# Hybrid DeltaNet and GLA block, merge stage: order of rows, head norms and first up part changed

## What is computed

```python
def merge(o_a, z, o_b, gate, dtype):
    y_a = _merge_heads(_rms_norm(o_a, gdn_norm)) * jax.nn.silu(z)
    y_b = _merge_heads(_rms_norm(o_b, gla_norm)) * jax.nn.silu(gate)
    return (jnp.concatenate([y_a, y_b], axis=-1).astype(w_out.dtype) @ w_out).astype(dtype)
...
x = x + m_lat[2] * y_lat
h_lat = _modulate(_rms_norm(x, norm2[i]), m_lat[3], m_lat[4])
x = x + m_lat[5] * _conv_ffn(h_lat, w_up[i], ffn_conv[i], ffn_conv_b[i], w_down[i], True)
```

## Time and profile before

| what | us |
|---|---|
| median of three runs | 1724.89 |
| lowest and highest | 1723.58, 1726.42 |
| the profiled execution | 1726.9 |
| its span, first to last instruction | 1725.2 |
| PE busy in it | 1642.6 |
| DVE busy | 1217.6 |
| ACT busy | 556.3 |
| POOL busy | 429.1 |

### The profile page before, as it was taken

One profiled execution on the slowest core, in us unless ns is written; L12 is line 12 of the kernel. 1 busy time (PEld: TensorE's weight loads), 2 busy tenths in 40 slices (PEclk: granted clock), 3 DMA queues, 4 the chain that ended last, 5 costly groups with the idle time before them and its releaser, 6 DMA issues.

```text
span 1725.2 us, 20820 instructions
## 1 busy us (share of the span) xinstructions
PE 1642.6 (95%) x8237; PEld 1221.3 (71%) x8237; DVE 1217.6 (71%) x1751; ACT 556.3 (32%) x888; POOL 429.1 (25%) x420
## 2 busy tenths in 40 slices
PE   7999999999999969999899799999999999999997
PEld 2544555886689956565577688888888888787886
DVE  2568877599456658888765469899988888534535
ACT  1533233454043322222544422222222222322432
POOL 4000000220123336656213423333333333200000
PEclk9999999989899979999999899999999999999999
DMA  9275554864388640000312311111111111532342
GB/s 337 79 267 155 162 183 151 250 164 128 86 246 235 195 158 13 25 13 25 128 58 78 116 42 47 47 49 49 49 50 49 49 49 38 219 98 98 98 134 85
DMA packets 202172, 194.23 MB, mean 113 GB/s; under 512 B 41045, under 2 KB 156063, under 8 KB 201948
## 3 DMA queue, kind: packets, MB, share of 16 engines
q1 hardware_dynamic: 194972, 187.40, 34.5%
q10 hardware_dynamic: 6816, 5.24, 1.0%
q0 software_dynamic: 288, 0.27, 0.0%
HBM read 150.77 MB, written 42.11 MB: 112 GB/s over the span
## 4 chain that ended last, share of the span: by engine, by line
PE 49%; DVE 6%; ACT 3%; DMA 2%; issue 2%; POOL 2%; SPq 0%; ACTq 0%; POOLq 0%; DVEq 0%
PE PS L2024 9%; PE PS L2026 9%; PE PS L2028 9%; PE PS L2061 4%; PE PS L2063 4%; PE PS L2065 4%; PE PS L1906 4%; PE PS L1920 2%; DVE Qbd L2306 2%; DMA ogb<-og_spill 1%; POOL xr L1866 1%; PE PS L1963 1%; DVE AT L2322 1%; DVE wolo L2418 1%; DVE oss L2270 0%
## 5 line engine op out<-in xcount | busy, mean ns | idle before, releaser
L2450 DVE SCALAR_TENSOR_TENSOR acc<-PS,fcol,acc 128x945 f32<-128x945 f32 (+2 forms) x176 | 215.2, 1223 | 35.4 <-ACT acc L2147 29.8
L2450 DVE SCALAR_TENSOR_TENSOR act<-PS,fcol,act 128x945 f32<-128x945 f32 (+2 forms) x176 | 215.2, 1223 | 21.6 <-ACT act L2147 16.2
L2024 PE MATMUL PS<-h2hi,whi 128*128 128x512 f32 x704 | 219.9, 390 | 0.0
L2026 PE MATMUL PS<-h2lo,whi 128*128 128x512 f32 x704 | 219.6, 389 | 0.0
L2028 PE MATMUL PS<-h2hi,wlo 128*128 128x512 f32 x704 | 219.6, 389 | 0.0
L389 PE MATMUL PS<-hT,wq 128*128 128x512 f32 (+1 forms) x432 | 163.8, 539 | 0.0
L1860 POOL TENSOR_TENSOR wlo<-wu,whi 128x1024 fp32r<-128x1024 f32 x44 | 106.4, 2420 | 215.8 <-ACT whi L2140 215.7
L2024 PEld LDWEIGHTS PS<-h2hi,whi 128*128 128x128 f32 x704 | 132.4, 188 | 27.4
L2026 PEld LDWEIGHTS PS<-h2lo,whi 128*128 128x128 f32 x704 | 132.4, 188 | 27.4
L2028 PEld LDWEIGHTS PS<-h2hi,wlo 128*128 128x128 f32 x704 | 132.3, 188 | 27.6
L2461 DVE TENSOR_TENSOR wrlo<-wr,wrhi 128x1024 fp32r<-128x1024 f32 x41 | 50.2, 1225 | 129.6 <-ACT wrhi L2221 129.6
(11 more groups left out here) (283 smaller groups left out, 2869.6 us busy)
## 6 DMA issues: line engine op xcount, KB each, us to landing
wm<-in_w_mod_dram SPq DMA_DIRECT2D x24, 1024.0 KB, 7.9
wu<-in_w_up_dram SPq DMA_DIRECT2D x44, 512.0 KB, 3.8
wr<-in_w_down_dram SPq DMA_DIRECT2D x44, 512.0 KB, 3.5
wq<-in_w_in_dram SPq DMA_DIRECT2D x12, 512.0 KB, 9.0
gdn_x_image<-ztile SPq DMA_DIRECT2D x10, 516.0 KB, 9.9
gdn_xt_image<-ztile SPq DMA_DIRECT2D x10, 516.0 KB, 8.3
GR<-gdn_gc_rows SPq DMA_DIRECT2D x20, 256.0 KB, 5.3
gdn_w_image<-Wm SPq DMA_DIRECT2D x20, 256.0 KB, 4.9
```

The costliest lines, as they stand in the source:

```text
L2024: pe.matmul(PS[:, b + half, :], whi[k][u][:, kk, :], h2hi[:, 4 * half:4 * half + 4, kk, :], start=(kk == 0), stop=False)
L2026: pe.matmul(PS[:, b + half, :], whi[k][u][:, kk, :], h2lo[:, 4 * half:4 * half + 4, kk, :], start=False, stop=False)
L2450: tp = v.scalar_tensor_tensor(out=t_[:, r0:r1, c0:c1], in0=up[:, r0 + dr:r1 + dr, c0 + dc:c1 + dc], scalar=tap_col(j, k, f), in1=t_[:, r0: ...
```

## The change

SP asks for the row of tile t+1 in step t, one step sooner than before; the first pair of up weights is asked for one step sooner too. On ACT and DVE the head norm is taken apart. ACT: squares(t+2) stands behind h2_evac(t-2) and ahead of h2hi and of second(t-1); the root of tile t+2 stands behind second(t-1). DVE: the sums of tile t+2 (reduced) stand ahead of second(t-1); reciprocal and scalings (scaled) between gated_y(t+1) and y_low(t+1). Since osq then holds the head squares while second(t-1) runs, the squares of x1, of which only the sum is used, are written to og2's rows 3 and 4 (the first two tiles of the order, read by then) for t < 5 and to osq from there. POOL makes the low part of the first up weights ahead of h2lo(5) and not behind it. PE does up part 0, k = 0, token half 0, ahead of turn2(7), and k = 1 behind it.

```diff
@@ -1745,10 +1745,11 @@
                 sp.wait_ge(s_o2[0], NL)
                 x_row(0)
                 x_row(1)
+                og_row(2)
                 for t in range(2, NL + 2):
-                    if t < NL:
-                        og_row(t)
-                    if t == NL:
+                    if t + 1 < NL:
+                        og_row(t + 1)
+                    if t == NL - 1:
                         sp.wait_ge(s_5y, NL)
                         w_pair(0)
                     sp.wait_ge(s_5a, t - 1)
@@ -1870,10 +1871,10 @@
                     g.tensor_tensor(h2lo[:, TORD[t], :, :], h2T[:, TORD[t], :, :], h2hi[:, TORD[t], :, :], ALU.subtract).then_inc(s_hlp, 1)
                 for t in range(NL):
                     add(t)
+                    if t == NL - 2:
+                        low(0)
                     if t:
                         h2_low(t - 1)
-                    if t == NL - 2:
-                        low(0)
                 low(1)
 
                 def gated(f):
@@ -2014,7 +2015,6 @@
                     project(t, 1)
                     if t:
                         turn2(t - 1)
-                turn2(NL - 1)
 
                 def up(f, k, halves_of):
                     u = f % 2
@@ -2030,9 +2030,11 @@
                     return mm
                 pe.wait_ge(s_hlp, 5)
                 pe.wait_ge(s_5x, NL - 1)
-                for k in range(2):
-                    pe.wait_ge(s_wl[k], 1)
-                    up(0, k, (0,))
+                pe.wait_ge(s_wl[0], 1)
+                up(0, 0, (0,))
+                turn2(NL - 1)
+                pe.wait_ge(s_wl[1], 1)
+                up(0, 1, (0,))
                 pe.wait_ge(s_hlp, NL - 1)
                 pe.wait_ge(s_hlv, 1)
                 for k in range(2):
@@ -2153,8 +2155,8 @@
                     sq = osq if t else osq0
                     a.activation(sq[:, 0:H, :].rearrange("p h n -> p (h n)"), ogb[t % 2][:, :], ACT.Square)
                     a.activation(sq[:, H:2 * H, :].rearrange("p h n -> p (h n)"), og2[:, TORD[t], :], ACT.Square).then_inc(s_5q, 1)
-                    if t == 0:
-                        silus(0)
+
+                def root1(t):
                     a.wait_ge(s_5s, t + 1)
                     a.activation(ort[:, :], oss[:, :], ACT.Sqrt, scale=1.0 / P, bias=epsc[:, :]).then_inc(s_5r, 1)
 
@@ -2179,17 +2181,22 @@
                         ev = a.activation(h2T[:, TORD[t], k, :], PS[:, 4, k * P:(k + 1) * P], ACT.Identity,
                                           scale=gain[:, 2 * KT + k:2 * KT + k + 1], bias=mods[:, 3 * KT + k, 0:1])
                     ev.then_inc(s_5va, 1)
+
+                def h2_high(t):
                     a.wait_ge(s_5vv, t + 1)
                     a.wait_ge(s_5va, t + 1)
                     a.activation(h2hi[:, TORD[t], :, :], h2T[:, TORD[t], :, :], ACT.Copy).then_inc(s_hh, 1)
 
                 def second(t):
                     a.wait_ge(s_5a, t + 1)
-                    a.activation(osq[:, :, :].rearrange("p h n -> p (h n)"), xr[t % 2][:, :], ACT.Square,
+                    junk = og2[:, 3:5, :].rearrange("p h n -> p (h n)") if t < 5 else osq[:, :, :].rearrange("p h n -> p (h n)")
+                    a.activation(junk, xr[t % 2][:, :], ACT.Square,
                                  accum_out=ss2[:, :]).then_inc(s_5z, 1)
                     a.wait_ge(s_5z, t + 1)
                     a.activation(rt2[:, :], ss2[:, :], ACT.Sqrt, scale=1.0 / D, bias=epsc[:, :]).then_inc(s_5rt, 1)
                 squares(0)
+                silus(0)
+                root1(0)
                 gate_copy(2 * H - 1, 1)
                 a.wait_ge(s_o2[0], NL)
                 for k in range(4):
@@ -2198,21 +2205,28 @@
                 for k in range(4, KT):
                     w_high(k)
                 squares(1)
+                root1(1)
                 silus(1)
                 for t in range(NL):
                     if t >= 2:
                         h2_evac(t - 2)
+                    if t + 2 < NL:
+                        squares(t + 2)
+                    if t >= 2:
+                        h2_high(t - 2)
                     if t >= 1:
                         second(t - 1)
+                    if t + 2 < NL:
+                        root1(t + 2)
                     if t + 1 < NL:
                         y_high(t + 1)
-                    if t + 2 < NL:
-                        squares(t + 2)
                     if t == NL - 2:
                         high(0)
                 h2_evac(NL - 2)
+                h2_high(NL - 2)
                 second(NL - 1)
                 h2_evac(NL - 1)
+                h2_high(NL - 1)
                 high(1)
 
                 def high7(i):
@@ -2265,9 +2279,11 @@
                 v.wait_ge(s_s2[1], 1)
                 v.wait_ge(s_s2[0], 1)
 
-                def first(t):
+                def reduced(t):
                     v.wait_ge(s_5q, t + 1)
                     v.tensor_reduce(oss[:, :], (osq if t else osq0)[:, :, :], AX_X, ALU.add).then_inc(s_5s, 1)
+
+                def scaled(t):
                     v.wait_ge(s_5r, t + 1)
                     v.reciprocal(ors[:, :], ort[:, :]).then_inc(s_5i, 1)
                     v.wait_ge(s_5i, t + 1)
@@ -2347,7 +2363,8 @@
                                 q_args(l, (i + 1) * P)
                             q_factors(i + 1, 0)
                         if i == NL - 1:
-                            first(0)
+                            reduced(0)
+                            scaled(0)
                         merged(i, LEVELS)
                     if lat:
                         add_o(1, i, seed)
@@ -2416,19 +2433,23 @@
                 for k in range(KT):
                     v.wait_ge(s_woh, k + 1)
                     v.tensor_tensor(wolo[:, k, :], wo[:, k, :], wohi[:, k, :], ALU.subtract).then_inc(s_wolv, 1)
-                first(1)
+                reduced(1)
+                scaled(1)
                 for t in range(NL):
                     if t >= 1:
                         residual(t - 1)
                     if t >= 2:
                         h2_evac(t - 2)
+                    if t + 2 < NL:
+                        reduced(t + 2)
                     if t >= 1:
                         second(t - 1)
                     if t + 1 < NL:
                         gated_y(t + 1)
+                    if t + 2 < NL:
+                        scaled(t + 2)
+                    if t + 1 < NL:
                         y_low(t + 1)
-                    if t + 2 < NL:
-                        first(t + 2)
                 residual(NL - 1)
                 h2_evac(NL - 2)
                 second(NL - 1)
```

## The result

The changed kernel takes 1702.51 us (median of four runs, 1700.19 to 1706.34), the kernel before in the same rounds 1725.66 (1723.58 to 1727.31): ratio 0.9866, 95% interval 0.9844 to 0.9888, a gain of 23.15 us by the medians. The forecast was 1707.4, and the range began at 1704.3: faster, as forecast, but by more than the range held. One of the timings of the kernel before in the later rounds, 3368.02 us, was slow and is left out of every comparison.

The account below looks back on a forecast made before the run. Only the merge stage could move, its rounds bound by a ring including the row's DMA. Rounds less start loss 9.85 plus end 9.25 made 19.1 us, 17.5 with the low clock: from 1724.89 to 1707.4 us, range 1704.3 to 1712.0.

Parts of the forecast that it names:

- Who closes the ring: Merge stage rounds: the landing of the first scan's row (median 3.7 us) is a full member of the 15.17 us ring.
- The new round: Merge stage: with early rows and the head norm split, PE becomes the bound and a round takes 12.69 us.
- The start: First merge round: DVE's and ACT's added work makes PE's product of tile 1 2.1 us late.
- The end: Last merge turns: the first up part between them gains 9.25 us and leaves a hole of 0.55 us.
- The weight pair: First up weights, requested at about 942 us instead of 963.5: landing and POOL's new order are covered by margins.
- The clock behind the new hole: Behind the new hole at the merge stage's start the granted clock falls to 0.50, costing 1.6 us.
- rival (1): No low clock behind the new hole in the merge stage: 1705.8 us; chance 0.22.
- The range: Whole kernel: 1704.3 to 1712.0 us, from rival (1) less 1.5 us of run spread to the longer-round rival plus 1.
- Rival (4): Merge rounds: a late row holds the whole round, eating all gain at a landing of about 11.5 us; chance 0.03.

Follow-up runs that it names:

- changed again: The changed kernel without any edit, timed and profiled once more: 1705.52 us, ratio 0.9873 to the kernel before.
- turn ahead: Changed kernel, but PE does the last turn ahead of both first up parts, as before the change: 1711.55 us.
- row late: Changed kernel, but SP asks for each row of the first scan only in the round that needs it: 1720.34 us, ratio 0.9976.
- xn alone: Changed kernel, but DVE, not POOL, makes the low part of h2 of tile 6, behind xn(7): 1706.18 us.
- weight pair late: Changed kernel, but the first pair of up weights is asked for where it was before the change: 1708.09 us, one run.
- end only: Kernel before with only PE's end changed (an up part between the last two turns) and POOL's low weights ahead of h2lo(5): 1713.49 us.
- silus early: The kernel of xn alone, with ACT's four silus of the second half ahead of the root of tile 1: 1700.02 us, ratio 0.9868.
- yT ahead of the sums: Changed kernel, but in the first step DVE makes yT(1) and ylo(1), and ACT yhi(1), ahead of tile 2's sums, scalings and root: 1705.57 us, ratio 0.9878.
- rows only: Kernel before with only SP's order changed, the rows of the first scan asked for one tile sooner: 1712.40 us, ratio 0.9925.
- low weights early: The kernel of silus early, with the first two low parts of w_out on DVE ahead of ylo(0): 1700.72 us, ratio 0.9863.

## Why the prediction was right or wrong

**Who closes the ring.** Right: without the row's wait a round is 13.28, with the split 12.70 (12.69 forecast). ACT's wait for ogb is gone in all rounds, and so is PE's for ylo from tile 2 on.

**The new round.** Right to some tenths: from the product's end at 902.05 yT ends after 8.8 us (9.1 in the sum) and ylo after 11.3 (11.8), and DVE waits 1.42 us for the next product where I had a margin of 0.9.

**The start.** Right: 2.1 us, measured 2.07.

**The end.** Right: 9.25 in the sum, 9.0 alone; the hole 0.55 against 0.46, its part from POOL 0.4 against 0.46. The weight pair was rightly costed at nothing. It was asked for at 937.66, and the second token half began at 977.84: with the 3.47 us by which this execution was ahead, 941.1 and 981.3, as forecast (942, 981 to 983).

**The clock behind the new hole.** Wrong, the first term that failed: I took 1.6 us, and it was 0. Six executions with this hole of 1.7 us (changed, changed again, turn ahead, row late, xn alone, weight pair late) show no fall behind it. I took the fall from two holes of 2.06 and 2.19 us against one of 2.20 and counted them as draws. The count was short by one; the kernel before has a fourth such hole,

```profile
951.95 0.50 PE L1994 MATMUL PS<-wohi,yhi 128*128 128x512 f32 x1 [2.10 <-DVE ylo L2391]
```

and its turn comes at 959.14, 7.2 us later, as behind 921.68, and not 5.6 as behind 906.52: a fall. Nor are they draws in the merge stage: both executions of before, and "end only" with the same rounds, have the long rounds at the same tiles (turn to turn 16.7 and 16.7 us, 16.7 and 16.8, 16.8 and 16.6, from tile 4 to 5 and from 6 to 7). The new hole was also shorter than those, 1.7 us and not 2.1 to 2.2; whether it escaped the fall by its length or by its place is not shown. In "end only" a hole of 2.00 us ahead of 903.06 has no fall and one of 2.00 ahead of 948.45 has. With 0 in place of the 1.6 the sum was 19.1, rival (1), and the stage gave 18.9.

**The range.** Wrong, the second: I let only the merge stage move, and put 1.5 us below rival (1) for the runs' spread, from three runs that lay within 2.8 us. The stages ahead of the merge, unchanged, differ by 8 us between executions (867.0 to 875.2 over the eleven executions that share this code), and the kernel before ran from 1721.68 to 1731.52 us over all rounds. 1702.5 lies 3.3 us below rival (1), 1705.8, and the stage does not explain it (18.9 against 19.1): of the profiled gain, 3.5 us lie ahead of the stage, where the time at 0.50 was 54.6 us and not 64.9, and 0.9 behind it. Timed again, the same kernel took 1705.52 us, inside the range. So the mechanism was right, and that the first median fell outside the range was in part luck.

**Rival (4)** has an error in its sum. By the prediction's own terms its ring passes the forecast round by the whole gain, 17.5 / 5 = 3.5 us, at 16.2 us, a landing of 10.4 us and not 11.5, and rounds of 19.5 us would give 1707.4 + 5 x 6.8 = 1741 and not 1732.

**Behind the stage** 0.9 us more were gained in the profiled execution. The hand-over from up to down has a hole of 1.87 us before, 1.89 after. The stretches around it, before and after, columns as in the earlier trace rows:

```profile
1472.00:1480.00 8.00, 6.13 (x20) 4.65 (x19) 7.82 (x7) 3.95 (x5) 6.05 (x5) 0.79 1.02 390
```

```profile
1449.00:1457.00 8.00, 6.11 (x28) 4.72 (x27) 7.79 (x7) 4.00 (x5) 6.40 (x4) 1.00 0.99 374
```

The same hole is followed by a fall in one and not in the other. The down projection has a second such place, a hole of 2.12 to 2.31 us that ends when DVE has written yb. In the changed kernel and in "silus early":

```profile
1568.00:1576.00 8.00, 5.81 (x19) 4.61 (x19) 8.00 (x9) 2.92 (x5) 0.00 (x0) 0.79 0.22 66
```

```profile
1564.00:1572.00 8.00, 5.81 (x26) 4.79 (x26) 8.00 (x9) 2.90 (x5) 0.00 (x0) 1.00 0.20 66
```

These two places sort all thirteen executions by what they take behind the stage. With a fall at both it is 719.3 to 719.8 us (both of before, "yT ahead of the sums", "turn ahead of the up part", "row late"), with a fall at the second alone 718.1 to 718.4 (changed, changed again, "end only", "xn alone", "weight pair late"), and with none 716.7 to 716.8 ("rows only", "silus early", "low weights early"). So each fall is worth 1.2 to 1.5 us, in places that no edit touches.

**What stays open.** Stage and hand-over give 20.1 us. The medians say 23.15 in the first rounds and 21.0 in the second (1726.49, the median of the ten runs of before that count, less 1705.52); the intervals reach down to 19.3 and 18.1. The mean of all ten runs of the changed kernel, 1703.99, is 22.1 us below that of the 14 of before in the same rounds and 21.0 below that of all 37; resampling the runs gives 20.0 to 24.2 and 19.3 to 22.7 as an estimate. I have no sign of a further steady gain: the eleven values ahead of the stage do not sort by kernel (before 870.9, 875.2, end only 867.6; changed 867.4, 870.0). But that the last 1 to 3 us are chance is not shown by a count of executions large enough, whether the hand-over keeps its clock in the changed kernel by more than chance is not shown either, and why the clock falls in one execution of the scan and not in another is not known.

## What to carry to other kernels

A transfer that is asked for behind a step of the ring it feeds is a member of that ring, even a short one (here a landing of 3.7 us in a ring of 15.1). Here asking one turn sooner brought the round to 13.28 us, and laying the head norm beside the other chain brought it to 12.70, where the busiest engine sets the pace. Work that is ready and long (here 24 matmuls) belongs into the longest wait of the bound engine; here that move was worth 7.8 us of 18.9. Before giving a range, look at how far two executions of the unchanged kernel differ in the stages that the change does not touch: here 8 us against a margin of 1.5.

## What the runs showed of the hardware

The granted clock falls behind holes that are alike, or does not: a hole of 1.9 us at the hand-over has both in different kernels, and so has one of 2.1 to 2.3 us in the down projection, 1.2 to 1.5 us each. The hole of 1.7 us in the merge stage was never followed by a fall in six executions, though the clock had been at half for the eight transposes of 867.41 not long before it. Within one kernel a fall in the merge stage came in the same place in each execution. In the scan ahead of it the clock of a 60 us stretch went from 0.80 to 0.91 between executions, and over the eleven with the same program there the time at 0.50 ahead of the stage went from 54.6 to 75.1 us, while the start of the stage went from 867.0 to 875.2.
